# Both decodes of a hybrid layer as one stage over a ring of equal tiles

## The reference, cut to what matters

```python
# NSA (8 query heads, 2 key heads, ALiBi): three branches, gated and added
o_cmp = softmax(q . kc - slope * dist) . vc          # 127 compressed blocks
o_sel = softmax over the 16 best blocks of 64 rows   # cache_sel_k, cache_sel_v
o_win = softmax over the last 512 rows and the new   # state_win_k, state_win_v
o_nsa = g0 * o_cmp + g1 * o_sel + g2 * o_win
# FoX (8 heads, own keys): all 2048 past rows and the new
logits = q . k * scale + c_new(q) - c(key)           # c: running sum of log f
o_fox = softmax(logits) . v                          # cache_fox_k, _v, _logf
```

## Time and profile before

| | us |
|---|---|
| median of 3 runs (lowest, highest) | 1047.73 (1046.89, 1050.21) |
| the profiled execution | 1047.75 |
| its span | 1045.6 |
| busy TensorE, VectorE, ScalarE, GpSimd | 874.4, 538.8, 355.6, 143.2 |
| NSA decode, first product to the last | 373.6 to 478.6 |
| FoX decode, first transpose to the last value tile's arrival | 481.0 to 661.2 |
| first record of the merge | 676.5 |

### The profile page before, as it was taken

The page is one execution under the profiler, slowest core; times in us unless marked ns, Lnnn a source line. Parts: engine busy times, 40 slices in busy tenths (PEclk is TensorE's granted clock), DMA queues, the critical chain, the costliest instruction groups (busy, mean ns, idle before and its releaser), DMA issues. The chain is left out here.

```text
span 1045.6 us, 18213 instructions
## 1 busy us (share of the span) xinstructions
PE 874.4 (84%) x7327; PEld 726.5 (69%) x7327; DVE 538.8 (52%) x950; ACT 355.6 (34%) x605; POOL 143.2 (14%) x221
## 2 busy tenths in 40 slices
PE   2899358989999965556888987499997999999997
PEld 1789156878989943435666542299967898888885
DVE  5443558743433737374446230155565665665654
ACT  3322545533333322022234120153434434434431
POOL 0000300010220111412122433000000111111010
PEclk9999669999999977788899998899998999999999
DMA  5341483027322286645887999596804535535511
GB/s 194 114 166 56 137 243 132 1 99 165 139 105 82 81 306 268 222 161 211 314 320 283 371 426 419 177 287 161 303 9 155 166 122 165 197 120 177 184 40 54
DMA packets 95962, 191.68 MB, mean 183 GB/s; under 512 B 7418, under 2 KB 74778, under 8 KB 83514
## 3 DMA queue, kind: packets, MB, share of 16 engines
q1 hardware_dynamic: 80060, 87.45, 27.4%
q0 software_dynamic: 14544, 102.90, 25.4%
q10 hardware_dynamic: 1296, 0.45, 0.2%
HBM read 187.30 MB, written 7.64 MB: 186 GB/s over the span
## 5 line engine op out<-in xcount | busy, mean ns | idle before, releaser
L227 PE MATMUL banks<-tokens_turned_high,w_gates_high 128*128 128x288 f32 x320 | 95.8, 299 | 3.7 <-PEq L186 2.3
L229 PE MATMUL banks<-tokens_turned_high,w_gates_low 128*128 128x288 f32 x320 | 95.7, 299 | 0.0
L228 PE MATMUL banks<-tokens_turned_low,w_gates_high 128*128 128x288 f32 x320 | 94.3, 295 | 0.0
L958 PE MATMUL banks<-chunks_turned_high,cmp_w_high 64*128 64x256 f32 (+1 forms) x512 | 78.1, 298 | 5.3 <-DVE cmp_w_low L220 2.7
L1559 PE MATMUL banks<-consts_base,stream_rows 128*128 128x128 f32 x512 | 63.4, 286 | 14.8 <-DVE fox_keys_turned L1660 11.8
L958 PE MATMUL banks<-chunks_turned_low,cmp_w_high 64*128 64x256 f32 (+1 forms) x512 | 74.7, 285 | 0.0
L958 PE MATMUL banks<-chunks_turned_high,cmp_w_low 64*128 64x256 f32 (+1 forms) x512 | 74.5, 284 | 0.0
L1559 PEld LDWEIGHTS banks<-consts_base,stream_rows 128*128 128x128 f32 x512 | 60.1, 148 | 19.5 <-issue 17.6
L1672 ACT ACTIVATE fox_keys_turned<-banks 128x512 f32<-128x512 f32 x64 | 37.3, 596 | 96.0 <-PE banks L1636 58.4
L227 PEld LDWEIGHTS banks<-tokens_turned_high,w_gates_high 128*128 128x128 f32 x320 | 61.1, 191 | 4.8 <-issue 2.7
L220 DVE TENSOR_TENSOR chunks_turned_low<-banks,chunks_turned_high 128x512 fp32r<-128x512 f32 x64 | 41.1, 684 | 41.6 <-ACT chunks_turned_high L215 41.6
(11 more groups left out here) (417 smaller groups left out, 2078.0 us busy)
## 6 DMA issues: line engine op xcount, KB each, us to landing
w_up_gate<-in_w_up SPq DMA_DIRECT2D x12, 1024.0 KB
w_up_gate<-in_w_gate SPq DMA_DIRECT2D x12, 1024.0 KB
w_down<-in_w_down SPq DMA_DIRECT2D x12, 1024.0 KB, 5.0
w_in_slot<-in_w_in SPq DMA_DIRECT2D x8, 1424.0 KB, 6.1
w_gates<-in_w_in SPq DMA_DIRECT2D x16, 512.0 KB, 5.4
cmp_w<-in_cmp_w_k SPq DMA_DIRECT2D x4, 512.0 KB, 20.9
cmp_w<-in_cmp_w_v SPq DMA_DIRECT2D x4, 512.0 KB
win_k_rows<-in_state_win_k SPq DMA_DIRECT2D x8, 256.0 KB
```

Of the source, the lines that this page charges most:

```text
L227: nc.tensor.matmul(out, lh, rh, start=start, stop=False, **kw)
L228: nc.tensor.matmul(out, lh, rl, start=False, stop=False, **kw)
L229: return nc.tensor.matmul(out, ll, rh, start=False, stop=stop, **kw)
L958: ins = nc.tensor.matmul(c.ps[4 + g][:, 0:w], x[rows, half * CS + 4 * q + i, :], y[k % 2][rows, i, src], start=(q + i + half + part == 0), ...
```

## The change

- The two stages become one, `stage_decode`. A list, `decode_steps`, written out by hand, says in which order TensorE takes the steps of both jobs: 16 FoX key tiles of half 0, three NSA key tiles, the FoX probabilities, then FoX values of half 0 between FoX keys of half 1 with the NSA values of half 0 among them, the NSA keys of half 1, and last the values of half 1 of both. Each engine walks the same list.
- All cache rows go through one ring of 7 buffers of 1 MB, in the order of the list. A tile is released alone: a key tile when it is transposed, a value tile when it is multiplied. A tile of selected rows now holds a quarter of the rows of four sequences, in four gathers with 2 KB a row; window tiles are loaded by SyncE into the same ring.
- A FoX key tile is one step: 16 transposes, 4 copies into one of three buffers, 4 products. Rows of FoX logits are ordered by pair of heads, then sequence, and a column group is a pair of heads; the products of the four sequences add up in it. The bias is four products of 128 columns for four tiles.
- A FoX value tile is one step: its four slots go to the four column groups. After four tiles VectorE copies the sums and a product with `fold` adds the four groups up (8 folds). The probabilities are turned by a product with a permutation, `foxbatch`, instead of a transpose, so that they come out by sequence.
- Past forget gates are gathered, and their sums over slots made, by GpSimd in `stage_compress`; the first two ring tiles are gathered four steps before the end of that stage, the next two at its end.
- The block mask is folded into the distances, 512 columns once a half, so L1456 goes. The block choice is cut in four parts, laid between key tiles.
- The outputs are made before VectorE splits the merge weights.

```diff
@@ stage_heads, ScalarE
-                                ins = nc.scalar.activation(c.fqb[rows, j, :, (2 * j + g) * DS:(2 * j + g + 1) * DS], ...)
+                                for half in range(2):
+                                    lo = (j * 2 + half) * P
+                                    dst = c.fqb[rows, lo:lo + 160].rearrange("p (b x) -> p b x", x=40)[:, :, DS * g:DS * (g + 1)]
+                                    ins = nc.scalar.activation(dst, ps[rows, ...], ACT.Copy, scale=gain)
@@ stage_compress, GpSimd
+                if G == 1:
+                    for b in range(DB):
+                        nc.gpsimd.indirect_dma_start(c.past_logf[:, b]..., d["cache_fox_logf"]...)
...
-            pool.wait_ge(turned, NSTEP)
-            for b in range(4):
-                gather_sel_keys(c, 0, b)
+            pool.wait_ge(c.past_logf_in, 16 * DB)
+            for half in range(2):
+                link(nc.gpsimd.memset(after[:, SLOTS - 1], 0.0))
+                for s in range(SLOTS - 2, -1, -1):
+                    link(nc.gpsimd.tensor_tensor(by_row(after[:, s]), by_row(after[:, s + 1]), by_pair(lf[:, :, s + 1, :]), ALU.add))
+                link(nc.gpsimd.tensor_tensor(by_row(c.logf_total[:, half]), ...))
+            for n in range(4):
+                pool.wait_ge(turned, NSTEP - 4 if n < 2 else NSTEP)
+                gather_decode_rows(c, n)
@@
-def stage_nsa_decode(c):
-def stage_fox_decode(c):
+DEC_RING = 7
+def decode_steps():
+    return (fox(0, 0, 1) + [("sums", "both", 0, 0)] + new("nsa", 0) + fox(0, 2, 3) + new("fox", 0) + fox(0, 4) + score(0) + fox(0, *range(5, 16))
+            + nsa(0, 0, 1, 2) + probs(0) + vals(0, 0, 1) + nsa(0, 3) + vals(0, 2, 3) + nsa(0, 4)
+            + vals(0, 4) + fox(1, 0) + fold(0, 0) + vals(0, 5) + fox(1, 1) + vals(0, 6) + fox(1, 2) + vals(0, 7) + fox(1, 3) + new("fox", 1) + fold(0, 1)
+            + vals(0, 8) + fox(1, 4) + nsa_v(0, 0, 1, 2) + vals(0, 9) + fox(1, 5) + nsa_v(0, 3, 4) + vals(0, 10) + fox(1, 6) + nsa_v(0, 5)
...
+            + fox(1, 14) + nsa(1, 1, 2) + fox(1, 15) + nsa(1, 3, 4) + probs(1) + vals(1, 0, 1, 2, 3) + nsa_v(1, 0, 1, 2) + fold(1, 0)
+            + vals(1, 4, 5) + nsa_v(1, 3, 4) + vals(1, 6, 7) + nsa_v(1, 5, 6) + fold(1, 1) + vals(1, 8, 9) + nsa_v(1, 7) + vals(1, 10, 11, 12) + fold(1, 2)
+            + vals(1, 13, 14, 15) + fold(1, 3) + out("nsa", 1) + out("fox", 1))
+def gather_decode_rows(c, n):
...
+    table = c.d[f"cache_sel_{x}"][0].rearrange("n (r s) g h -> (n r) (s g h)", s=4)
+    for b in range(4):
+        c.nc.gpsimd.indirect_dma_start(c.stream[r][:, b * 4 * KVW:(b + 1) * 4 * KVW], None, table, ...)
+def stage_decode(c):
...
+            for n in range(4, len(ring)):          # GpSimd
+                if window(ring[n]):
+                    continue
+                if n >= R:
+                    release(pool, n - R)
+                gather_decode_rows(c, n)
...
+            turn(0)                                # TensorE
+            for s, (kind, job, half, i) in enumerate(steps):
+                if kind == "vals":
+                    fox_values(half, i).then_inc(products, 1)
+                if s + 1 < len(steps):
+                    turn(s + 1)
+                if kind == "keys":
+                    key_products(s, job, half, i).then_inc(products, 1)
...
+                    if b == 3:                     # key_products, FoX
+                        pe.wait_ge(bias_ready, 4 * half + k + 1)
+                        for q in range(4):
+                            nc.tensor.matmul(c.ps[4][:, q * P:(q + 1) * P], biasq[:, q, :], c.k("ident"), ...)
+                    for j in range(4):
+                        ins = nc.tensor.matmul(c.ps[4][32 * j:32 * j + 32, :], fox_q(c, j, half, b), kT[kbuf[s]][:, j, :], start=(b == 0), stop=(b == 3))
...
+                for q in range(4):                 # fox_values
+                    at = (4 * k + q) * P + 32 * b
+                    ins = nc.tensor.matmul(c.ps[6][32 * q:32 * q + 32, :], fpT[:, at:at + 32], tiles[slot[item]][:, q, :], start=(k == 0), stop=(k == 3))
...
+                return nc.tensor.matmul(c.ps[7][32 * b:32 * b + 32, :], c.k("fold"), acc[b % 2][:, :], start=False, stop=True)
```

More of the change, by code:

```diff
@@ L1256, in _, with landed @@
+        def landed(eng, item):
+            if window(item):
+                eng.wait_ge(window_in[item[0], item[2]], 64)
+            else:
+                eng.wait_ge(c.ring_in[slot[item]], arrived[ring.index(item)])
         @block.sync
         def _(sp):
[L1258 to L1266 removed]
@@ new lines, in _ @@
+            load_fox(sp)
+            load_nsa(sp)
+            load_select(sp)
+            for n, item in enumerate(ring):
+                if not window(item):
+                    continue
+                r, (kind, _, half, _) = n % R, item
+                release(sp, n - R)
+                for b in range(B4):
+                    src = d[f"state_win_{'k' if kind == 'keys' else 'v'}"][0, half * 4 + b].rearrange("(p s) g e -> p (s g e)", s=4)
+                    sp.dma_start(tiles[r][:, b, :], src).then_inc(window_in[kind, half], 16)
@@ L1535, in _ @@
+            sp.wait_ge(products, done[max(keys[-1], chunks[-1])])
+            for i in range(12, 16):
+                landed(sp, ("vals", "fox", 1, i))
             load_gates(c, sp, c.gates, c.gates_in, 0)
@@ new lines, in nsa_values @@
+            def nsa_values(s, half, i):
+                t, p = first[s], pT[pbuf[s]]
+                pe.wait_ge(copied[engine[t]], copies[t])
+                if i == 0:
+                    pe.wait_ge(nsa_taken, 7 * half + 7)
+                lo = P * (0, 1, 1, 2, 2, 2, 2, 2)[i]
+                own = i == 2 or i > 3
+                if own:
+                    item = ("probs", "nsa", half, max(i - 3, 0))
+                    landed(pe, item)
+                for q in range(4 if own else 1):
+                    for b in range(B4):
+                        if own:
+                            v = tiles[slot[item]][:, b, q * KVW:(q + 1) * KVW]
+                        elif i == 0:
+                            v = c.vc[:, half * 4 + b, :]
+                        else:
+                            new = c.kept_at["wv" if i == 1 else "sv"][0]
+                            v = c.kept[:, new:new + KVW]
+                        ins = nc.tensor.matmul(c.ps[5][32 * b:32 * b + 32, lo:lo + P], p[:, q * P + 32 * b:q * P + 32 * b + 32], v,
+                                               start=i in (0, 1, 3), stop=i == 0 or (i in (2, 7) and q == 3))
+                return ins
```

959 lines of the change are left out of this document (462 added, 497 removed).

## The result

| | before | after |
|---|---|---|
| median, us (runs) | 1048.97 (4) | 1035.17 (4; 1031.13 to 1039.46) |
| the profiled execution, its span | 1047.75, 1045.6 | 1031.13, 1029.0 |
| decode, first record to the last value tile | 287.7 | 272.8 |
| last value tile to the merge's first record | 15.3 | 10.9 |

The ratio is 0.987, with an interval of 0.9822 to 0.9917: 13.8 us faster, where 46.7 were forecast. 1035.2 lies outside the range of 972 to 1030.

A forecast was written before the change was run, and what follows sets the result against it. Neither TensorE nor transfers were full in decode; merging the stages would use each one's idle time, with TensorE setting the mixed part. 1047.75 less 44.6 (last tile earlier) and 2.7 (end) gave about 1001 us; forecast 988 to 1018, range 972 to 1030.

The forecast's parts named there:

- Moved ahead: Before decode: forget-gate gathers (10 us of GpSimd) and 34 small GpSimd operations (11 us) cost nothing; 3 us if cover fails.
- The tail: Decode from 195 us on: fourteen tiles still to issue, a selected one taking GpSimd 4.96 us; last tile at 243 us.
- The mixed part: From first to last key tile of half 1: TensorE sets the time, 109 us, against 96.7 us of transfers.
- wait before a product that follows values: Where FoX keys alternate with values: TensorE stands 1.05 us for the key copies before each key tile's products.
- a sign of being wrong: TensorE waiting for tiles in the mixed part would show the forecast wrong: transfer bound or GpSimd's issue.
- the 70.2 us of half 0: Decode's start to the third NSA key tile: 19 key tiles at 2.90 us plus smaller terms, 70.2 us.
- The allowance of 7 us for VectorE, cold tiles and clock: Within half 0: VectorE waits 4 us, first tiles without cover 1 us, lower clock at the start 2 us.
- the probabilities and first values: After the third NSA key tile: probabilities 4.3, five value tiles 4.8, two NSA key tiles 5.8, waits 1: 15.9 us.
- the end: After the last tile: output goes ahead of the merge-weight split, so 15.3 us become 12.6, 2.7 us won.
- Waits at every step: Rival, chance 0.20: each of 42 key tiles meets a 1.56 us wait; half gives 1027 us, the whole 1053; or GpSimd's issue, 1031.
- The transfer bound: Rival, chance 0.22: TensorE loses less, the ring never runs empty and transfers bound decode; 985 us, floor 972.
- The low clock: Rival, chance 0.06: TensorE stands at nearly every tile and the granted clock stays at 0.76; 1062 us, slower by 1.4%.

The follow-up runs named there:

- e5: Changed kernel with each selected tile filled by one gather of 8-KB rows, then three gathers of 128 tiny rows: 1036.39 us, ratio 0.9868.
- e1: Changed kernel with each selected tile filled by one gather of 8-KB rows instead of four of 2 KB (selected blocks wrong): 1005.99 us, ratio 0.9593.
- e7: e1's kernel with four GpSimd fills of a dead tile, some 0.95 us each, behind each selected tile's gather: 1011.98 us, ratio 0.9659.
- r1: The changed kernel itself, run again on a chip of the second kind: 1002.28 us, ratio 0.9735 to the kernel before.
- r2: Changed kernel with selected tiles as single gathers of 8-KB rows, one small gather behind each, on the second kind: 993.43 us, ratio 0.9649.
- e2: Changed kernel with the eight forget-gate gathers in compression issued two at a time behind four chunk groups: 1027.81 us, ratio 0.9801.
- e13: Changed kernel with selected tiles one batch each (48 gathers fewer), forget-gate gathers spread and two steps moved, on the second kind: 1007.47 us, ratio 0.9776.
- e6: e5's kernel with 16 rows instead of 128 in each of the three small gathers: 1041.38 us, ratio 0.9936.
- r4: e13's kernel run again beside the changed kernel, on the second kind: 1007.16 us, ratio 0.9782.

## Why the prediction was wrong

Two steps failed by the same omission. **"Moved ahead"** put the gathers of forget gates at nothing ("I cost all of it at nothing"). And the selected tile ("is now four of them: 4.96 us") was charged in **"The tail"** with GpSimd's time and in **"The mixed part"** with its bytes alone; that part took 127.2 us where 109 were forecast. What a train of gathers does to the other engines was in no term. On the first kind 48 gathers cost 30 us (e5 against e1), of which 6 to 9 are GpSimd's own time (e7; r1 against r2), and the train in compression cost 6 to 9 more (e2; r1's trace). The rows shown ahead of the prediction could not have told it: the earlier trace rows lists TensorE's waits alone. ScalarE's 21.1 us of "remote" and the train beside it were in the same profile.

Term by term, as forecast, on the first kind and on the second:

| | forecast | first kind | second kind |
|---|---|---|---|
| decode starts | 373.6 | 376.1 | 364.1 |
| to the third NSA key tile | 70.2 | 70.7 | 64.5 |
| to the end of value tile 4 | 15.9 | 18.9 | 18.9 |
| mixed part | 109 | 127.2 | 110.2 |
| to the last value tile | 48 | 56.0 | 56.4 |
| to the merge's first record | 12.6 | 10.9 | 10.8 |
| the profiled execution | 1001 | 1031.1 | 996.8 |

- **Right, by the second kind:** the mixed part (1.2 us off), with 0.8 us of wait before a product that follows values (1.05 forecast) and 1.06 for the bias (0.9). A key tile is 2.90 us (402.26 to 405.16 in the first profile), as in the earlier trace rows, against the 2.70 of the earlier trace rows. The Trainium skill (TensorEngine Tiling (Array Packing), Key Properties) says that TensorE drains at each change of tiling mode; that the 0.20 us are this drain no run here shows. The transfers were closer to being the bound than forecast: their share is 0.98 in the mixed part, and TensorE waits 2.7 us there for FoX keys, which the prediction had named as a sign of being wrong.
- **Right for the wrong reason:** the 70.2 us of half 0. The allowance of 7 us for VectorE, cold tiles and clock was not needed (64.5 us on the second kind); on the first kind the stretch with a train of eight at 415 to 424 took its place.
- **Too small on both kinds:** the probabilities and first values, 15.9 for 18.9; and the tail, 48 for 56, so here the standstills are not the main part. From its start to its first gather are 10.9 us on the second kind (557.75 to 568.67) and 7.8 on the first, where 5.3 were forecast; the 3 us between them are the clock (eight records of the probabilities take 2.08 us in the one and 1.16 in the other). From that gather to the last tile are 45.4 and 48.1 us, where 42.5 were forecast. On the second kind GpSimd issues 26 gathers without a pause from 568.67 to 599.91, and the last tiles arrive 2.5 us apart, as forecast.
- **Too large:** the end, by 1.7 us. Counted nowhere was the gap ahead of decode, which shrank from 5.07 to 1.67 us and on the first kind paid back 3.4 of the 8.9 us that compression lost.
- **The rivals.** "Waits at every step" gave 1027 to 1031 and landed nearest, but its mechanism was GpSimd's issue time holding up tiles, and the runs price that at 6 to 9 us. The transfer bound's 985 us and its floor of 972 leave out the 2.7 us of the end; by their own terms they are 982 and 970. The low clock (0.92 in the mixed part, 1.00 on the second kind with the same order of work) came with the standstills, and it was a large part of their price: the same 901 records keep TensorE busy for 100.9 us instead of 91.0. So up to 9.9 of the 17.0 us between the two mixed parts are slower records, and the rest is standing.

That the second kind gave 1002.3 is no success of the forecast. It had been made against 1047.75; against 1030.5 the gain is 28.2 us. And term by term its profile (996.8) meets 1001 by luck: decode starts 9.5 us early and half 0 is 5.7 us short, against 3.0, 1.2 and 8.4 us of overrun. Between the kinds the kernel before differs by 18.5 us (1049.0 and 1030.5) and the changed one by 32.9 (1035.2 and 1002.3). The difference, 14.4 us, is what the changed kernel gave back of its gain of 28.2. The 32.9 us are close to the 34.2 by which the forecast was missed. The priced trains make 27 to 33 of them (21 to 24, and 6 to 9 in compression); both were never taken out together on the first kind, so that they are the whole of it is argued, not shown.

## What to carry to other kernels

Count gathers, not only their bytes and GpSimd's time, and look at how many stand in a row: on some chips VectorE and ScalarE, and in places TensorE, stood still around trains of four and more, and splitting 16 tiles into four gathers each cost some 30 us of a 1035-us kernel, against some 9 where nothing stood still. Waits marked "issue" or "remote" on several engines at once need not be noise; look at what the one engine that still runs is doing. And compare only runs of one chip: here the same two kernels stand at 0.987 on one kind and at 0.9735 on the other, and e13, the version that is built to spare gathers, falls behind the changed kernel on the second.

## What the runs showed of the hardware

- Between the two kinds the kernel before differs by 1.7% (1047.4 to 1049.0 in three comparisons, 1028.8 to 1031.0 in three others). The start of decode, with the train of compression as it is, lies at 374.9 to 381.8 us on the first kind and at 364.1 to 369.5 on the second, in kernels that are the same up to there.
- Around a train of gathers on the first kind VectorE and ScalarE stand for up to 8 us (e6), and ScalarE for 12.6 us (compression), in steps of some 1.43 us where they move at all (541 to 544 us). 16 or 128 rows in the added gathers make it no smaller.
- What holds them is not known. The profile names nothing; GpSimd's time (e7), bytes (e1) and rows (e6) are excluded as the main cause, and no run changed the chip's kind. The expectation of e2 speaks of the other engines' instructions being starved; no run tests that. Whether the kind is one of the chip or of what surrounds it at the time was not tried either. Nor is the second kind free of such waits: r4 has a single one of 5.3 us before L1465.
